# New costs and finer pieces for the order planner of a four-layer decoder trunk, and its window attention put under the same planner

## The reference

```python
for layer in range(4):
    h = rms_norm(x, g)
    proj = h @ w_in                      # 4608, 1792 or 2560 columns
    # HGRN, 8 heads of 128: S_t = diag(f_t) S_{t-1} + k_t v_t^T, o_t = S_t^T q_t,
    #   f = lb + (1-lb)*sigmoid(f_raw), k = 1-f, in chunks of 64 tokens,
    #   then rms_norm(o) * silu(gate)
    # SWA, 16 query heads and 2 key heads of 64, window 128:
    #   scores of a block of 128 queries with its own and the previous block of keys,
    #   softmax with a learned sink, times v
    xa = cross attention of 4 heads into 256 memory tokens
    x = x + concat(mix, xa) @ w_out
    x = x + square(relu(rms_norm(x) @ w_up)) @ w_down
```

## Time and profile before

| | |
|---|---|
| median of 2 runs | 4960.35 us (4959.08 to 4961.62) |
| the profiled execution | 4958.07 us, span 4956.5 us on its slowest core |
| cores | 4939.9 to 4956.5 us, granted clock 0.885 to 0.891 |
| busy | PE 3946.5 us (80%), DVE 2092.2 (42%), ACT 1999.5 (40%), POOL 1193.2 (24%) |
| chain that ended last | PE 60%, ACT 15%, issue 10%, DVE 7%, POOL 4%, DMA 3% |

### The profile page before, as it was taken

The page is one execution under the profiler, slowest core; times in us unless marked ns, Lnnn a source line. Parts: engine busy times, 40 slices in busy tenths (PEclk is TensorE's granted clock), DMA queues, the critical chain, the costliest instruction groups (busy, mean ns, idle before and its releaser), DMA issues.

```text
span 4956.5 us, 68109 instructions; the slowest of 8 cores (4939.9 to 4956.5 us)
## 1 busy us (share of the span) xinstructions
PE 3946.5 (80%) x20936; PEld 1898.5 (38%) x20936; DVE 2092.2 (42%) x3510; ACT 1999.5 (40%) x4126; POOL 1193.2 (24%) x1196
## 2 busy tenths in 40 slices
PE   3666668899947778899979945899986666689998
PEld 2333334344412434344434412344433333344444
DVE  1665542433365542433430023333355555334334
ACT  2566654211136763311153346211136666631111
POOL 1010110244413421344400000144421111013442
PEclk9787779999979569999989968999998777899999
DMA  5010111222210001232210000232220111011222
GB/s 154 27 35 18 35 30 39 73 90 85 69 43 26 2 14 47 69 102 73 81 35 18 18 0 26 65 94 81 68 69 18 35 35 35 26 60 52 84 70 94
DMA packets 123758, 259.34 MB, mean 52 GB/s; under 512 B 7824, under 2 KB 33552, under 8 KB 123408
## 3 DMA queue, kind: packets, MB, share of 16 engines
q1 hardware_dynamic: 123408, 255.00, 16.6%
HBM read 246.58 MB, written 8.39 MB: 51 GB/s over the span
## 4 chain that ended last, share of the span: by engine, by line
PE 60%; ACT 15%; issue 10%; DVE 7%; POOL 4%; DMA 3%; ACTq 1%; DVEq 0%; POOLq 0%; SPq 0%
PE p L446 59%; ACT t L459 14%; DVE t L471 5%; POOL t L462 3%; PE p L449 2%; DVE t L462 2%; DMA t<-x 1%; DMA t<-wkv 1%; ACTq L97 1%; DMA t<-wup 1%; POOL t L578 1%; DMA t<-wdn 0%; DMA y<-t 0%; DMA t<-mem 0%; ACT L459 0%
## 5 line engine op out<-in xcount | busy, mean ns | idle before, releaser
L446 PE MATMUL p<-t 128*128 128x512 bf16 (+5 forms) x20360 | 3847.6, 354 | 662.4 <-ACT t L459 399.2
L446 PEld LDWEIGHTS p<-t 128*128 128x128 bf16 (+2 forms) x20360 | 1813.3, 104 | 2687.1 <-issue 1172.8
L462 DVE TENSOR_TENSOR t<-p,t 128x512 f32<-128x512 f32 (+3 forms) x1736 | 1112.9, 642 | 2205.5 <-PE p L446 1327.1
L459 ACT ACTIVATE t<-p 128x512 f32<-128x512 f32 (+4 forms) x1536 | 798.1, 537 | 1922.4 <-PE p L446 1509.4
L459 ACT ACTIVATE t<-t 128x512 f32<-128x512 f32 (+8 forms) x2161 | 1008.2, 493 | 651.0 <-DVE t L462 364.1
L462 POOL TENSOR_TENSOR t<-t 128x512 bf16<-128x512 f32 (+4 forms) x748 | 726.7, 985 | 1577.3 <-DVE t L471 769.9
L578 POOL CAST t<-t 128x1024 bf16<-128x1024 f32 x442 | 470.3, 1064 | 2070.8 <-PE p L446 1406.0
L449 PE MATMUL p<-t 128*128 128x128 f32 x576 | 119.4, 356 | 337.4 <-POOL t L462 264.3
L459 ACT ACTIVATE t<-p,t 128x512 f32<-128x512 f32 (+2 forms) x408 | 234.5, 585 | 314.8 <-PE p L446 303.5
L471 DVE SCALAR_TENSOR_TENSOR t<-t 128x512 bf16<-128x512 f32 (+1 forms) x400 | 296.1, 743 | 97.7 <-ACT t L459 70.7
L462 DVE TENSOR_TENSOR t<-t 128x512 f32<-128x512 f32 (+5 forms) x411 | 272.8, 668 | 132.0 <-ACT t L459 103.3
(11 more groups left out here) (9 smaller groups left out, 7.6 us busy)
## 6 DMA issues: line engine op xcount, KB each, us to landing
t<-wup SPq DMA_DIRECT2D x128, 512.0 KB, 4.4
t<-wdn SPq DMA_DIRECT2D x128, 512.0 KB, 4.0
t<-win SPq DMA_DIRECT2D x106, 512.0 KB, 4.0
t<-wout SPq DMA_DIRECT2D x48, 512.0 KB, 3.6
t<-wkv SPq DMA_DIRECT2D x32, 512.0 KB, 4.1
t<-x SPq DMA_DIRECT2D x16, 512.0 KB, 3.8
y<-t SPq DMA_DIRECT2D x16, 512.0 KB, 2.7
t<-mem SPq DMA_DIRECT2D x8, 512.0 KB, 4.1
```

The costliest lines, as they stand in the source:

```text
L446: P.op("pe", lambda e: e.matmul(out, lhsT, rhs, start=start, stop=stop), reads, writes, inc)
L459: P.op("act", lambda e: e.activation(out, in_, func, **kw), reads, writes)
L462: P.op(eng, lambda e: e.tensor_tensor(out, a, b, op), reads, writes)
```

## The change

`op` takes a cost, and the helpers for matmuls, activations and two kinds of DVE and POOL products give one that depends on the size; where none is given, the number of `COST` stands. The planner adds 0.15 instead of 0.1 between the instructions of a chain. The forget, gate and query projections are written in two halves with a `yield` between them, the value projection in four parts with a `yield` behind each. The attention units of SWA go through `pipeline_gen` instead of `pipeline`, with yields inside, and take their PSUM banks from the halves A (0 to 3) and B (4 to 7) instead of all eight in turn. No instruction is added or removed, and none gets another size.

```diff
-    def op(self, eng, fn, reads=(), writes=(), inc=True):
+    def op(self, eng, fn, reads=(), writes=(), inc=True, cost=None):
         if self.log is not None:
-            self.log.append(eng)
+            self.log.append((eng, cost))
...
     def MM(...)
+             cost=0.06 + 0.00045 * int(np.prod(rhs.shape[1:])))
     def ACT(...)
+             cost=0.25 + 0.0008 * int(np.prod(out.shape[1:])))
     def TT(...)
+             cost=(0.1 + 0.0012 * int(np.prod(out.shape[1:]))) * (1.6 if eng == "pool" else 1.0))
     def STT(...)
+             cost=0.1 + 0.0012 * int(np.prod(out.shape[1:])))
...
-                for eng in P.log:
+                for eng, cst_ in P.log:
                     start = max(ch[1], teng[eng])
-                    teng[eng] = start + COST[eng]
-                    ch[1] = teng[eng] + 0.1
+                    teng[eng] = start + (COST[eng] if cst_ is None else cst_)
+                    ch[1] = teng[eng] + 0.15
...
+    def proj_gen(wt, wtt, c0, g, pool):
+        b = nb(pool)
+        for kc in range(8):
+            MM(pb[b][:], wt[:, kc, c0:c0 + 128], hT[:, kc, gs(g)], kc == 0, kc == 7, [wtt, hTt[g]], [pbt[b]])
+            if kc == 3:
+                yield
+        return b
...
     def sA1(k):
-            bf = proj_fm(wt, wtt, 128, g, "A1")
+            bf = yield from proj_gen(wt, wtt, 128, g, "A1")
     def sA1g(k):
-            bg = proj_fm(wt, wtt, 384, g, "A1g")
+            bg = yield from proj_gen(wt, wtt, 384, g, "A1g")
     def sA2(k):
-            bq = proj_fm(wt, wtt, 0, g, "A2")
+            bq = yield from proj_gen(wt, wtt, 0, g, "A2")
...
             for i in range(4):
                 for kc in range(8):
                     MM(pb[bv]...)
-            yield
+                yield
...
     def c1(u):
-                b = nb()
+                b = nb("A")
...
                 TT("pool" if par == 0 else "dve", e[:, par, lo:2, :], e[:, par, lo:2, :], swam[:, lo:2, :], ALU.mult,
                    [et[par], cstbt], [et[par]])
+                yield
     def c2(u):
-            bn = nb()
+            bn = nb("B")
...                                      # the eight matmuls
+            yield
             ACT(dn, pb[bn][:, 128:256], AF.Ln, [pbt[bn], smallt], [dnt], bias=esk[:, c:c + 1])
             ACT(dn, dn, AF.Exp, [dnt], [dnt], scale=-1.0)
+            yield
             TT("dve", mixT[:, c, n * 128:(n + 1) * 128], pb[bn][:, 0:128], dn, ALU.mult, [pbt[bn], dnt], [mixt[c][n]])
-        pipeline(128, c1, c2)
+        pipeline_gen(128, c1, c2)
```

More of the change, by code:

```diff
@@ L445, in MM @@
             inc = stop
-        P.op("pe", lambda e: e.matmul(out, lhsT, rhs, start=start, stop=stop), reads, writes, inc)
+        P.op("pe", lambda e: e.matmul(out, lhsT, rhs, start=start, stop=stop), reads, writes, inc,
+             cost=0.06 + 0.00045 * int(np.prod(rhs.shape[1:])))
     def TRN(out, in_, ident, reads, writes, inc=True):
@@ L458, in ACT @@
             kw["accum_out"] = accum
-        P.op("act", lambda e: e.activation(out, in_, func, **kw), reads, writes)
+        P.op("act", lambda e: e.activation(out, in_, func, **kw), reads, writes,
+             cost=0.25 + 0.0008 * int(np.prod(out.shape[1:])))
     def TT(eng, out, a, b, op, reads, writes):
-        P.op(eng, lambda e: e.tensor_tensor(out, a, b, op), reads, writes)
+        P.op(eng, lambda e: e.tensor_tensor(out, a, b, op), reads, writes,
+             cost=(0.1 + 0.0012 * int(np.prod(out.shape[1:]))) * (1.6 if eng == "pool" else 1.0))
     def TS(eng, out, a, s1, s2, op0, op1, reads, writes):
@@ L470, in STT @@
     def STT(out, a, s, b, op0, op1, reads, writes):
-        P.op("dve", lambda e: e.scalar_tensor_tensor(out, a, s, b, op0, op1), reads, writes)
+        P.op("dve", lambda e: e.scalar_tensor_tensor(out, a, s, b, op0, op1), reads, writes,
+             cost=0.1 + 0.0012 * int(np.prod(out.shape[1:])))
     def CP(eng, out, in_, reads, writes):
```

## The result

The ratio of the changed kernel's time to that of the kernel before is 1.0163, with a 95% interval of 1.0122 to 1.0204: slower by 60 to 101 us. The forecast was 5055 us, +1.9%. The median over all 12 runs, 5176 us against 4963.5, is not the measure of the change: in most of these runs the cores of one die or both had a lower granted clock, which happens to either kernel, and the ratios in this document leave such runs out. The lowest run is 5046.72 us, and the profiled execution has spans of 5035 to 5045 us.

The account below looks back on a forecast made before the run. HGRN and SWA were taken as bound by chains through in-order queues. The profiled 4958 us +60 (HGRN) +35 (SWA) = 5053, with the median 2 us above: 5055 us, 1.9% slower; range 4950 to 5135.

Parts of the forecast that it names:

- (a): HGRN: forget projection ends behind 19 units of 512 columns instead of 9, ACT starts at 6.46 against 4.10: +2.36 us.
- (b): HGRN: first state update S1 no longer stands behind sgt, 3.85 behind ACT's start instead of 4.81: -0.96 us.
- (c): HGRN, S1 to keb: sgt now inside and S6 to S8 ahead of keb, 3.14 becomes about 4.95: +1.8 us.
- (d): HGRN, keb to next BS: sta7, bo and square finish before POOL; 5.10 becomes 2.8 to 3.3: -2.1 us.
- the prediction's own formula: HGRN: ACT's start behind BS is r+(19-r/0.427)x0.2133+0.26 = 0.5r+4.31 us.
- r: HGRN: time behind BS when PE's upper clock level returns; 3.0 to 5.8 us, taken as 4.3.
- SWA, forecast 1.73 a unit: SWA: a one-unit loop replaces two interleaved ones; 1.45 becomes 1.73 us, +0.28 x 127 = +35 us, bounds 0 and +51.
- The clock did not stay up: First rival, not slower: split projections keep PE fed and the clock at the upper level; 4931 us, chance 0.20.
- did not stay away: Rival: clock never back in time, HGRN +186 and SWA +51 us, 5195 us; chance 0.13.
- both orders changed: Against the rival that the planner's HGRN order doesn't change, leaving SWA alone: 4993 us, chance 0.05.

Follow-up runs that it names:

- experiment 4: Kernel before with the new costs and the 0.15 alone in HGRN, whole projections, SWA as before; lowest run 4984.4 us.
- experiment 5: Kernel before with a fixed HGRN order: sta7, S8 and output products ahead of the transposes, square and BS ahead of k2t; lowest run 4872.4 us.
- experiment 6: Kernel before with the fixed short-tail HGRN order plus the changed kernel's projection split on PE alone; ratio to before 0.9983, lowest 4950.5 us.
- experiment 11: Kernel with HGRN as changed and SWA as before, plus keb ahead of S6 on DVE; ratio 0.9952, lowest 4944.0 us.
- experiment 8: Kernel before with SWA's second stage two units behind the first instead of one, three score buffers instead of two; ratio 0.9956, lowest 4931.8 us.
- experiment 7: Kernel before with both mask products of an SWA unit on DVE, order as before; ratio 0.9950, lowest 4938.6 us.
- experiment 10: Changed kernel with four output matmuls on either side of SWA's second score pair; ratio 1.0122, lowest 5028.2 us.

## Why the prediction was right

**The orders.** The planner's output worked was right in every row that the trace shows, in both stages. That the total hardly missed (+95 forecast, +88.6 between the profiled spans) is in part luck, as two errors of opposite sign stand in it: some 30 us too many in HGRN and some 30 too few in SWA.

The four terms, read over about 110 steps of each kernel (cores 1, 3 and 5, both layers; F is ACT's first exponential of the forget gate):

| us | step | BS to F (a) | F to S1 (b) | S1 to keb (c) | keb to BS (d) |
|---|---|---|---|---|---|
| before | 17.31 | 3.88 | 4.87 | 3.17 | 5.39 |
| changed | 17.74 | 5.97 | 3.80 | 4.94 | 3.03 |
| forecast for changed | 18.29 | 6.46 | 3.85 | 4.95 | 2.8 to 3.3 |
| experiment 4 | 17.76 | 3.88 | 6.35 | 4.50 | 3.03 |
| experiment 5 | 15.63 | 3.42 | 5.24 | 3.17 | 3.81 |
| experiment 6 | 17.16 | 5.62 | 4.65 | 3.10 | 3.80 |
| experiment 11 | 17.07 | 5.90 | 3.78 | 3.58 | 3.80 |

**(a) The later forget projection, forecast +2.36, measured +2.09.** ACT starts 5.57 behind BS in the step above, 6.90 in the step behind it (426.96 less 420.06), and 5.97 on average. By the prediction's own formula that is r=3.3 on average (2.4 to 5.2) where I took 4.3, and this is nearly all by which the step of 18.3 was missed. Why the clock is back at one time or another is not shown. PE works on bo and the transposes right up to BS now, where before it had stood idle for 0.94, but that does not explain it: in experiment 4 it does so too, with whole projections, and the mean start is the 3.88 of before. Experiment 6 has the term by itself: +2.20 in the wait, +1.5 in the step.

**(b) S1 ahead of sgt, forecast -0.96, measured -1.07.**

**(c) From S1 to keb, forecast +1.8, measured +1.77.** Experiment 11 took most of it out and gained 0.7 a step.

**(d) From keb to BS, forecast 2.8 to 3.3, measured 3.03.** Experiments 4 and 5 show the same gain under another order. The gain is 2.36 and not 2.1, because the step of rows 2, with 5.10, had a shorter tail than the mean, as it had a longer wait (4.10 against 3.88): one step stood for all.

Sum: +2.09-1.07+1.77-2.36=+0.43; the scans say +0.5. So the mechanism held in all four terms, and what was off in HGRN is the size of (a): 5.97 instead of 6.46, 0.5 us a step.

**SWA, forecast 1.73 a unit, measured 2.01.** The loop was the right one: e1, mask on DVE, half of pv, sc1, e1. Its first half was shorter than assumed: mask at 0.48 behind e1 (0.43) and 0.29 long (0.42). Its second was longer: from the mask's end, 1705.03, to the next e1, 1706.26, are 1.23 us, for which the sum had 0.1+0.54+0.2=0.84. The weight loads place the excess. From the second half of pv to the scores' weights are 0.57 (1705.15 to 1705.72) for four matmuls of 0.107, 0.14 more than they take. From there to ACT's start are 0.54, where the sum had 0.31: it counted five of the six matmuls, which is 0.11, and the other 0.12 is in the turn or in the way from PE to ACT, which the rows do not separate. In the order of before the same turns lay inside PE's slack. The Trainium skill, "TensorEngine Tiling (Array Packing)", Key Properties, says that a change of tiling mode drains TensorE; the 0.14 ahead of the scores' weights is of that kind, but no run here isolates it. It is a term that the forecast left out.

**The mask's price.** Two products of the same shape take 571 ns beside POOL and 295 alone. The Trainium skill, "SBUF — State Buffer", Who interferes with whom, says that a DVE instruction with two SBUF inputs and a GpSimd one that reads SBUF exclude each other; the earlier trace rows agree in kind, but DVE's mask ended 0.14 behind POOL's there, where full exclusion and 0.29 of work would give 0.29.

**The rivals.** The clock did not stay up (0.79 in HGRN, 0.50 in SWA) and did not stay away, and both orders changed. The 4 us pause of PE that spoke against the first is there: 4.56 ahead of bo.

## What to carry to other kernels

Where queues are written by a planner, work its order out for one steady step, find the one chain that closes the step, price each exchange on that chain only, and take the starting values as means over many steps. Better costs in the planner did not find that chain here (experiment 4). An instruction that waits for a slow partner should not stand ahead of one that closes the step: moving the last scaled state and the output matmuls ahead of the transposes, and the square ahead of the copy k2t, was worth 50 us a layer (experiment 5). For a loop of short units, a second stage two units behind instead of one cost one more buffer here and removed the loop (experiment 8).

## What the runs showed of the hardware that was not expected

- A DVE product of 256 bf16 columns takes 571 ns beside a POOL product and 295 alone, and moving POOL's share to DVE made the stage faster (1.45 to about 1.33 us a unit, ratio 0.9950; experiment 7).
- Twelve matmuls of 128 columns at the lower clock level, eight with weights of 64 columns and four of 64 rows, fit into 1.20 us with the heads' matmuls side by side and take 1.84 us with each head's apart and twice the turns between the two shapes (experiments 8 and 10).
- The upper clock level comes back at another time in each step of one kernel: ACT's first exponential starts 5.5 to 6.9 us behind BS in the changed kernel and 3.5 to 4.1 before, and neither PE's pause ahead of bo nor its work right up to BS tells which (experiments 4 and 5).
